# A hybrid decoder step: the swap of rotary embedding moved to VectorE, retention products by head, prompt attention from the last block of queries to the first

## The reference

```python
def rope(x, pos):
    ...
    x1, x2 = x[..., :half].astype(jnp.float32), x[..., half:].astype(jnp.float32)
    return jnp.concatenate([x1 * cos - x2 * sin, x1 * sin + x2 * cos], -1).astype(x.dtype)

def retention_chunkwise(q, k, v, s0, chunk):
    ...
    def step(s, xs):
        qc, kc, vc = xs
        a = jnp.einsum('bihd,bjhd->bhij', qc, kc) * inner
        o = jnp.einsum('bhij,bjhd->bihd', a, vc) + jnp.einsum('bihd,bhde->bihe', qc, s) * q_dec
        s = s * c_dec + jnp.einsum('bjhd,bjhe->bhde', kc * k_dec, vc)
        return s, o
```

## Time and profile before

| | us |
|---|---|
| median of 3 runs | 2009.65 (2005.47 to 2010.34) |
| profiled execution | 2008.16 |
| span of its trace, first to last instruction | 2006.4 |
| TensorE busy in the span | 1792.1 |
| VectorE busy | 777.8 |
| ScalarE busy | 589.7 |

### The profile page before, as it was taken

The page is one execution under the profiler, slowest core; times in us unless marked ns, Lnnn a source line. Parts: engine busy times, 40 slices in busy tenths (PEclk is TensorE's granted clock), DMA queues, the critical chain, the costliest instruction groups (busy, mean ns, idle before and its releaser), DMA issues. The chain is left out here.

```text
span 2006.4 us, 30938 instructions
## 1 busy us (share of the span) xinstructions
PE 1792.1 (89%) x11561; PEld 1560.1 (78%) x11561; DVE 777.8 (39%) x1499; ACT 589.7 (29%) x1246; POOL 171.3 (9%) x249
## 2 busy tenths in 40 slices
PE   4999999995799669999979938999999999999993
PEld 3988889895664645555549928999999999999993
DVE  4233233122015257766653294322332232223226
ACT  5212213111010146766652243311321132023211
POOL 1000000013243300000000041000000000000120
PEclk8999999998899758999998958999999999999996
DMA  7111111124875500000004012111111111111122
GB/s 267 36 39 44 29 36 39 32 74 96 204 206 165 152 0 1 1 1 1 1 22 137 11 74 74 52 42 42 51 43 42 52 42 42 52 43 42 42 106 84
DMA packets 171923, 126.38 MB, mean 63 GB/s; under 512 B 12102, under 2 KB 162971, under 8 KB 171379
## 3 DMA queue, kind: packets, MB, share of 16 engines
q1 hardware_dynamic: 140034, 88.70, 15.1%
q0 software_dynamic: 8752, 25.93, 4.3%
q10 hardware_dynamic: 23040, 10.50, 2.1%
HBM read 112.80 MB, written 16.47 MB: 64 GB/s over the span
## 5 line engine op out<-in xcount | busy, mean ns | idle before, releaser
L225 PE MATMUL psum<-act_hi,whi 128*128 128x344 f32 x1608 | 525.6, 327 | 26.7 <-DVE wlo L257 26.7
L225 PE MATMUL psum<-act_lo,whi 128*128 128x344 f32 x1608 | 516.9, 321 | 0.0
L225 PE MATMUL psum<-act_hi,wlo 128*128 128x344 f32 x1608 | 516.7, 321 | 0.0
L225 PEld LDWEIGHTS psum<-act_hi,whi 128*128 128x128 f32 x1608 | 305.2, 190 | 35.4 <-issue 34.1
L225 PEld LDWEIGHTS psum<-act_lo,whi 128*128 128x128 f32 x1608 | 305.0, 190 | 1.0
L225 PEld LDWEIGHTS psum<-act_hi,wlo 128*128 128x128 f32 x1608 | 305.0, 190 | 0.0
L225 PE MATMUL psum<-hidden_hi,whi 128*128 128x344 f32 x768 | 247.5, 322 | 11.4 <-DVE hidden_lo L1968 8.6
L225 PE MATMUL psum<-hidden_lo,whi 128*128 128x344 f32 x768 | 246.6, 321 | 0.0
L225 PE MATMUL psum<-hidden_hi,wlo 128*128 128x344 f32 x768 | 246.5, 321 | 0.0
L252 ACT ACTIVATE whi<-wraw 128x1024 fp32r<-128x1024 f32 x99 | 104.4, 1054 | 271.5 <-PE psum L225 251.9
L257 DVE TENSOR_TENSOR wlo<-wraw,whi 128x1024 fp32r<-128x1024 f32 x99 | 121.2, 1224 | 124.5 <-ACT whi L252 123.4
(11 more groups left out here) (349 smaller groups left out, 2218.6 us busy)
## 6 DMA issues: line engine op xcount, KB each, us to landing
wraw<-in_w_up SPq DMA_DIRECT2D x32, 512.0 KB, 4.1
wraw<-in_w_down SPq DMA_DIRECT2D x32, 512.0 KB, 3.9
wraw<-in_w_in SPq DMA_DIRECT2D x27, 512.0 KB, 3.8
h_features<-mixed_then_h SPq DMA_DIRECT2D x8, 516.0 KB, 2.6
h_again<-h_features SPq DMA_DIRECT2D x1, 4128.0 KB, 13.2
x_rows<-in_x_prompt SPq DMA_DIRECT2D x4, 1024.0 KB, 9.6
dec_pages<-in_cache_sel_k SPq DMA_DIRECT2D x64, 64.0 KB, 3.1
dec_pages<-in_cache_sel_v SPq DMA_DIRECT2D x64, 64.0 KB, 3.1
```

Of the source, the lines that this page charges most:

```text
L225: last = pe.matmul(out, w[:, kt, :], x[:, kt, :], start=(kt == 0 and n == 0), stop=(kt == KT - 1 and n == 2))
```

## The change

The swap leaves TensorE: VectorE multiplies each group of 32 partitions by the sine, read at the source's partitions, and writes the product to the neighbouring group of 32, so that four instructions take the place of the permutation product and of the one sine product. The sign in the sine table moves accordingly, the permutation matrix leaves the constants, and TensorE's waits on the swap go. VectorE waits for ScalarE's copy of the chunk instead of the swap. `make_kv`, `make_outer` and the states hold the two heads on their own partitions only (64 columns instead of 128), `outputs` does both heads' value products and then both heads' state products, and the decoded state is one instruction. In prompt attention the list of steps takes the blocks from 7 down to 0, and the waits and `split_q` count by place in that order.

```diff
@@ constants
-_COLS = [("ident", P), ("perm", P), ("center", P), ("ones", P), ("causal", P), ("winlow", P),
+_COLS = [("ident", P), ("center", P), ("ones", P), ("causal", P), ("winlow", P),
...
-    put("sin", np.sin(ang) * np.where(p % HD < half, -1.0, 1.0)[:, None].astype(np.float32))
+    put("sin", np.sin(ang) * np.where(p % HD < half, 1.0, -1.0)[:, None].astype(np.float32))
@@ projection
-        states = m.place("ret_states", [P, NB, P], F32, o + 12288)
+        states = m.place("ret_states", [P, NB, HD], F32, o + 12288)
...
-            def swap_halves(j, x, t):
-                pe.wait_ge(w.bank_free, w.evacuated(4 * j + x, t))
...
-                pe.matmul(ps[:, 5, 0:TN], m.c("perm"), (qT, kT)[x][j % 2][:, chunk(t)], start=True, stop=True).then_inc(swapped, 1)
...
             def make_kv(j):
                 pe.wait_ge(k_copied, 2 * j + 2)
                 for i in range(NB):
-                    last = pe.matmul(ps[:, 6 + i // 4, (i % 4) * P:(i % 4 + 1) * P], k_tok[:, i, :], v_tok[:, i, :], start=True, stop=True)
+                    for h in range(2):
+                        rows = slice(h * HD, (h + 1) * HD)
+                        last = pe.matmul(ps[rows, 6 + i // 4, (i % 4) * HD:(i % 4 + 1) * HD], k_tok[:, i, rows], v_tok[:, i, rows],
+                                         start=True, stop=True)
...
                 for h in range(2):
-                    last = pe.matmul(ps[:, 3 + h, :], kv_dec[:, 0, :], v_diag[:, 4 * h:4 * h + 4, :], start=True, stop=True)
+                    rows = slice(h * HD, (h + 1) * HD)
+                    last = pe.matmul(ps[rows, 3, :], kv_dec[:, 0, rows], v_diag[:, :, rows], start=True, stop=True)
                 last.then_inc(outer_made, 1)
...
                 for b in range(2):
                     i = 2 * pair + b
-                    for h in range(2):
-                        rows = slice(h * HD, (h + 1) * HD)
-                        out = ps[rows, 6 + i // 4, (i % 4) * P:(i % 4 + 1) * P]
-                        last = pe.matmul(out, v_tok[:, i, rows], aT[pair % 2][:, h, b, :], start=True, stop=(i == 0))
-                        if i:
-                            last = pe.matmul(out, states[rows, i - 1, rows], qd[rows, i * P:(i + 1) * P],
-                                             start=False, stop=True)
+                    halves = [slice(h * HD, (h + 1) * HD) for h in range(2)]
+                    out = [ps[rows, 6 + i // 4, (i % 4) * P:(i % 4 + 1) * P] for rows in halves]
+                    for h, rows in enumerate(halves):
+                        last = pe.matmul(out[h], v_tok[:, i, rows], aT[pair % 2][:, h, b, :], start=True, stop=(i == 0))
+                    for h, rows in enumerate(halves if i else ()):
+                        last = pe.matmul(out[h], states[rows, i - 1, :], qd[rows, i * P:(i + 1) * P], start=False, stop=True)
                 last.then_inc(out_made, 1)
...
-                pe.wait_ge(swap_read, min(6 * (j + 2), 24))
...
             def rope(j, x, t):
...
-                dve.wait_ge(swapped, k + 1)
+                dve.wait_ge(w.bank_free, w.evacuated(4 * j + x, t))
                 if k >= 2:
                     dve.wait_ge(roped, 2 * k - 2)
-                dve.tensor_tensor(tmp[:], ps[:, 5, 0:TN], m.c("sin")[:, chunk(t)], ALU.mult).then_inc(swap_read, 1)
+                for a in range(4):
+                    rows, to = slice(32 * a, 32 * a + 32), slice(32 * (a ^ 1), 32 * (a ^ 1) + 32)
+                    dve.tensor_tensor(tmp[to], tile[rows], m.c("sin")[rows, chunk(t)], ALU.mult).then_inc(crossed, 1)
+                dve.wait_ge(crossed, 4 * k + 4)
                 dve.tensor_tensor(tile, tile, m.c("cos")[:, chunk(t)], ALU.mult).then_inc(roped, 1)
-                dve.wait_ge(swap_read, k + 1)
                 dve.wait_ge(roped, 2 * k + 1)
                 dve.tensor_tensor(tile, tile, tmp[:], ALU.add).then_inc(roped, 1)
...
-                for h in range(2):
-                    rows = slice(h * HD, (h + 1) * HD)
-                    dve.scalar_tensor_tensor(s_new[rows], s_in[rows], m.c("gamma")[rows, j:j + 1],
-                                             blocks(ps[rows, 3:5, :])[:, :, rows], ALU.mult, ALU.add).then_inc(dec_state, 1)
+                dve.scalar_tensor_tensor(s_new[:], s_in[:], m.c("gamma")[:, j:j + 1],
+                                         ps[:, 3, :].rearrange("p (b f) -> p b f", f=HD), ALU.mult, ALU.add).then_inc(dec_state, 1)
@@ prompt attention
-        steps = [(i, g, r) for i in range(NB) for g in range(G) for r in range(R)]
+        ORDER = [NB - 1 - n for n in range(NB)]
+        steps = [(i, g, r) for i in ORDER for g in range(G) for r in range(R)]
...
                 if g == 0 and r == 0:
-                    pe.wait_ge(q_lo, 2 * i + 2)
+                    pe.wait_ge(q_lo, 2 * ORDER.index(i) + 2)
...
-            def split_q(i):
+            def split_q(n):
+                i = ORDER[n]
```

More of the change, by code:

```diff
@@ L85, in constants @@
     put("ident", np.eye(P))
-    perm = np.zeros((P, P))
-    perm[(p // HD) * HD + (p % HD + HD // 2) % HD, p] = 1.0
-    put("perm", perm)
     put("center", np.eye(P) - (p[:, None] // HD == p[None, :] // HD) / HD)
@@ L446, in stage_project @@
         p_dst = io["ret_state_prompt"][0, 0]
-        swapped, swap_read, roped = s("swapped"), s("swap_read"), s("roped")
+        crossed, roped = s("crossed"), s("roped")
         v_turned, k_turned, dec_turned = s("v_turned"), s("k_turned"), s("dec_turned")
@@ L592, in _ @@
                 w.multiply_chunk(pe, 4 * turn + slot // 3, slot % 3)
-                if turn < 4 and 1 <= slot <= 6:
-                    swap_halves(turn, (slot - 1) // 3, (slot - 1) % 3)
                 if slot == 0 and turn >= 2:
@@ L608, in _ @@
                 elif slot == 4:
-                    pe.wait_ge(dec_state, 2 * j + 2)
+                    pe.wait_ge(dec_state, j + 1)
                     scores(j, 0)
@@ L732, in make_states @@
                 for i in range(NB):
-                    kv = ps[:, 6 + i // 4, (i % 4) * P:(i % 4 + 1) * P]
+                    kv = ps[:, 6 + i // 4, (i % 4) * HD:(i % 4 + 1) * HD]
                     if i % 4 == 0:
@@ L847, in _ @@
                     rows = slice(h * HD, (h + 1) * HD)
-                    pool.dma_start(p_dst[2 * j + h], states[rows, NB - 1, rows]).then_inc(state_stored, 16)
-                pool.wait_ge(dec_state, 2 * j + 2)
+                    pool.dma_start(p_dst[2 * j + h], states[rows, NB - 1, :]).then_inc(state_stored, 16)
+                pool.wait_ge(dec_state, j + 1)
                 for h in range(2):
@@ L1575, in _, with split_q @@
         def _(dve):
-            def split_q(i):
+            def split_q(n):
+                i = ORDER[n]
                 for e in range(2):
                     rows, other = slice(e * HD, (e + 1) * HD), slice((1 - e) * HD, (2 - e) * HD)
-                    dve.wait_ge(q_hi, 2 * i + e + 1)
+                    dve.wait_ge(q_hi, 2 * n + e + 1)
                     dve.tensor_tensor(q_split[i % 2][other, :, e, :], m.nqT[rows, :, i * P:(i + 1) * P],
```

## The result

The changed kernel takes 1959.09 us (median of four runs, 1956.9 to 1966.03) beside 2008.55 for the kernel before on the same chip: ratio 0.9763, 95% interval 0.9742 to 0.9784. Forecast were 1965.5 and a range of 1950 to 1984. The profiled execution after is the longest of its runs, 1966.03 us with a span of 1964.4, so lengths of stages are compared between profiles, and times between medians.

What follows compares the result with a forecast made beforehand. TensorE, busy 89% of the span, was taken as the bound. Projection 31.3 us (13.9 + 14.0 + 0.8 + 2.6) plus attention 12.8 (7.3 + 4.5 + 4 - 3) made 44.1 us, giving 1965.5 us, range 1950 to 1984.

Steps and rivals of the forecast that it cites:

- Swap, 13.9: Projection: 24 swap products of 0.58 us leave TensorE, which never waits in a turn, saving 13.9 us.
- Cover, 1.3 us at slot 4: Projection turns: VectorE finishes the decoded state about 1.3 us before TensorE needs it in slot 4, so its added work is hidden.
- The rival of VectorE as the bound: Projection: at 0.9 us a swap product VectorE makes TensorE wait from slot 4 on, losing 18 us, 1983 us; chance 0.08.
- `outputs`, 14.0: Projection: pairing heads by shape cuts a block in `outputs` from 1.44 to 0.94 us, 14.0 us over 28 blocks.
- The rival that halves don't overlap: Projection: two heads' products don't run side by side, so `outputs` and `make_outer` gain nothing, 1982 us; chance 0.07.
- term (c): Attention, blocks 0 and 1: value products of larger blocks fill 4 of the 5.5 us that TensorE waits.
- (a): Attention, block 0: at full clock it takes 21 us instead of 28.3, saving 7.3 us.
- (b): Attention, block 2: 9 us at clock 0.50 with TensorE busy go at full clock, saving 4.5 us.
- (d): Attention start: the large blocks now meet the low clock, 5 to 6 us at 0.50, costing 3 us.
- Rival 1: Attention: the new order brings nothing, the clock staying low through the first six steps, 1977 us; chance 0.15.
- rival 4: Attention: the low clock holds on in large blocks 7 and 6, slower than before, up to 2053 us; chance 0.03.
- Rival 5: Attention: more gain than forecast, block 0 at 15 us and no low-clock start, 1955 us; chance 0.05.

Runs made afterwards that it cites:

- swap alone: Kernel before with only the swap moved from TensorE to VectorE, heads together in the products as before: 1991.14 us, ratio 0.9915.
- the doubled products: Changed kernel with VectorE doing each of the four swap products of a rope step twice: 1980.55 us, ratio 0.987 beside 2007.3 for the kernel before.
- the heads alone: Kernel before with only the products by head (`make_kv`, `make_outer`, `outputs`, narrow states), swap still on TensorE: 1980.16 us, ratio 0.9858.
- the order alone: Kernel before with only the attention's query blocks taken from 7 down to 0, projection as before: 1999.62 us, ratio 0.9955.

## Why the prediction was right, and where its terms were off

The time was right, and by the mechanism named: products leave the engine that never waits in the projection. That it came so close is in part luck: the projection gave 8.7 us more than forecast and the attention 5.3 less, and the two largely cancel.

- **Swap, 13.9.** Measured 14.0 by stage (swap alone). VectorE's step was forecast at 3.35 us and took 3.15, with 0.54 from product to product. The rule that the forecast cites from the Trainium skill's page "VectorE: DVE Perf Modes", section "Two Vector instructions with no wait between them", agrees here: 0.54 at a length of 0.51, against 0.43 on all partitions.
- **Cover, 1.3 us at slot 4.** 1.6 by the timeline after, 1.9 by the doubled products. The rival of VectorE as the bound is a real mechanism, shown with a price, and stood 0.1 to 0.2 us a product away.
- **`outputs`, 14.0: the mis-sized term.** The step was "two heads side by side in one shape cost 0.11 for the second". It costs 0.00; the stage shows 20.2 with that edit alone. The 0.58 for three value products in the earlier trace rows was read as a product and two seconds; it is a pair behind a change of shape (0.37) and a third product that begins a new pair of the same shape (0.21). The trace before had it: the first two of these three products start within 0.01 us of each other. The bound of 14.0 given there was too low for the same reason. The rival that halves don't overlap falls.
- **`make_kv` and `make_outer`, 0.8 and 2.6.** 1.15 and 1.07 long, against 1.95 and 1.98. These are lengths; by stage the heads alone give 25.5, and less 20.2 for `outputs` these two are 5.3 together, not 3.4. No run separates them.
- **Attention, 12.8.** 7.5 by stage. The step that failed is term (c), 4 us of filled waits: TensorE's idle time did not fall but rose, from 18.7 us (326.6 - 307.9) to 19.9. In blocks 0 and 1 it did fall, from the 5.5 of the forecast to 3.2, but block 7, whose first steps have no value products beside them, went from 2.0 to 5.7.
- **The attention's clock: a total near the forecast from terms that were off.** Low time went from 40.9 to 19.0 us, which gives 10.9 where TensorE has work; terms (a), (b) and (d), those on the clock, had 7.3 + 4.5 - 3 = 8.8. But the low clock of the old order cost 20.4, not 11.8, and that of the new order 9.5, not 3. Term (d), the start, was 5.4 (block 7 at 0.88): the clock rises soon and falls once more behind a wait. The fall among the small blocks at the end, some 8 us of low time in blocks 1 and 0 and what follows them, cost 4 that were not in the sum, as the last paragraph of the forecast had said would show it wrong. Term (a), block 0 in 21 us at full clock, did not come about: with the products that it carries the block takes 25.5, at 0.91. By this account the order works through the clock alone: 10.9, less 1.2 of idle time and 2.2 by which the busy time at full clock comes out higher than before (299.2 - 9.5 against 307.9 - 20.4), which is not explained.

Rival 1 (order worth nothing) and rival 4 (slower) are out by the order alone, 10.2 us; the large blocks 6 to 3 stand at 1.00. Rival 5's time (1955) is near the one measured, but not for its reason: the start was low, and block 0 did not take 15 us.

Open: why the clock falls behind one wait of about 1 us and not behind another, and why stages without an edit differ by several us in low time between profiles. Through this the attention in the old order ran 323.0 to 328.2 us in five profiles.

## What to carry to other kernels

Where the bottleneck engine never waits, count every product that leaves it, and take an unseen pair from rows of the same shape by subtracting start to start, not by sharing out a sum. Group products by shape: here the change of shape cost 0.15 us and the second tile of a pair nothing. On a busy TensorE a wait of 4 us cost some 3 us more here, behind it, through the clock, so the cover of a helper engine is worth more than its own length.

## What the hardware showed that was not expected

- Two products of 64 x 64 in different rows and columns of the array, writing one bank of PSUM, take 0.37 us with a change of shape and 0.22 (0.59 - 0.37) without, as long as one alone.
- A wait of 3.7 to 4.5 us at full clock was followed, three times of three, by some 7 us at 0.50 with TensorE busy throughout; with the wait filled by useless work this did not happen in two of the three places.
- Making TensorE faster again brought out waits that its slow clock had hidden: 8.7 us of clock came back as 3.2 of stage.
